# The routing of a mixture-of-experts layer: its work moved between the last tiles of the projection before it, and expert 0 chosen first

## The chip, the cores and the metric

The kernel runs on one core of a Trainium2 chip, as one launch. The metric is the device time of that launch in microseconds, as a median of several runs. TensorE multiplies, VectorE and ScalarE do the elementwise work, the SP queue issues nearly all loads, and GpSimd issues the indirect gathers and scatters of the expert loop. The engines meet at semaphores: an instruction raises a count, another engine's next instruction waits for it.

## What is computed

The reference is a decoder trunk of two layers with a prompt of 256 tokens and 8 samples of 4 tokens, so 288 tokens of 1024 values. Layer 0 has two kinds of attention and a dense SwiGLU, layer 1 two recurrent mixers and a mixture of experts. The change lies between the output projection of layer 1's mixers and its experts. The reference there, shortened:

```python
hp = hp + y                                   # output projection of the mixers, 1536 -> 1024
xn = rms_norm(hp, norm_ffn_odd)
logits = jnp.einsum('btd,de->bte', xn, w_router).astype(jnp.float32)
top_val, top_idx = lax.top_k(logits, TOP_K)   # 2 of 8
top_w = jax.nn.softmax(top_val, axis=-1)
gate = jnp.sum(jax.nn.one_hot(top_idx, N_EXPERTS) * top_w[..., None], axis=-2)
for e in range(N_EXPERTS):
    out = out + gate[..., e:e + 1] * swiglu(xn, we1[e], we3[e], we2[e])   # 1024 -> 3584 -> 1024
```

Everything is float32. Each expert has 44 MB of weights, and the eight of them take more than half of the kernel's time.

## The kernel before

**Layout.** `residual` holds the 288 tokens as columns, in eight chunks of 128 channels. The router and the experts want tokens as rows, in three tiles (`TILES`): 128, 128 and 32 tokens. PSUM has eight banks of 512 columns.

**The projection (`gemm_rows`, L644).** The last call, `_out_odd`, adds up over six halves of weights into eight output tiles, one for each chunk and bank. In the last half every tile m is finished in turn: six matmuls of 288 columns, about 0.8 us, then VectorE adds bank m to `residual` (L745) and raises `added`. `head.follow` (L588) is called behind each tile; before the change it does nothing until the last tile, m = 7.

**The router's head (`RouterHead`, L511).** Behind the last tile TensorE issues, in this order: the scores of chunks 0 to 4 (`score`, L558: 8 experts as weights, 288 tokens as columns, into bank 0), the turns of chunks 0 to 3 (`turn`, L579: three transposes each, to token rows in banks 1 to 3), scores 5 and 6, turns 4 to 6 (banks 4 to 6), then `finish_scores` (L568): for each token tile the seven chunks' partial scores, which VectorE has copied out (`keep_part`), times an identity, plus the last chunk directly. Turn 7 and five warm matmuls follow, which compute nothing that is used. Every float32 matmul is two instructions in the trace, a transpose is one.

**The statistics.** ScalarE squares the turned rows as they come (`square`, L603, 512 columns for each half and token tile, with a running sum). The norm's scale is needed as 1/sqrt(mean), from two ScalarE instructions, logarithm and exponential (L3431, L3433).

**The choice (`choose`, L622).** VectorE copies the logits, compares each expert with each other one (128 x 192 elements), breaks ties by order, counts who is above, and marks the two best in `chosen`. TensorE turns `chosen` into ranks within each expert (L3235 to L3237, matmuls with a triangle and with ones). VectorE makes `at_first` from the ranks of expert 0 (L3284, L3287): for each token a row with 1/rms at its slot among expert 0's 96 slots.

**The picks (L3247).** Expert 0's tokens are not gathered from memory: TensorE multiplies `at_first` with the turned rows. For each of three groups of 32 slots, and each token tile, four matmuls of 256 columns write the four quarters of a bank. VectorE multiplies each group with the norm's gain and transposes it (L3292, L3293) to `item_x`, and raises `half_x` or `xg_ready`.

**The experts (`stage_experts`, L2970).** `open_item` (L3149) begins expert 0 with the first two chunks of its first weight (L3162), group by group, and counts the tokens of all experts (`count`, L3167) ahead of the third group. From the count VectorE works out a table of items for the other experts (L3303 on). `item` (L3172) then runs up products (L3186) and down products (L3202) for each item. Weights come through rings of 8 up slots and 7 down slots: the SP queue issues a load when TensorE has freed its slot (`free_up`, `free_down`). Six up blocks of expert 0 are loaded far ahead (`EARLY_UP`); four down blocks when the last tile is done (`head.all_read`); up slots 6 and 7, and all that SP issues behind them, when `head.chose` and the squares are there (L3084, L3085).

The order on each engine is written by hand, as the order of the calls.

Of the kernel before, what the change touches and what calls it, by code (L numbers as in the profile page):

```python
# [21 lines left out]
ALU = mybir.AluOpType  # L22
ACT = mybir.ActivationFunctionType
# [487 lines left out]
class RouterHead:  # L511


    def __init__(self, k, work, early_up):
# [8 lines left out]
        self.junk = [work[:, n:n + 512] for n in (512, 1024, 1536)]  # L523
# [26 lines left out]
    def weigh(self, dve):  # L550
        gain = self.k.vec[:, VEC["norm_ffn_odd"]:VEC["norm_ffn_odd"] + DC].unsqueeze(2).broadcast_to([P, DC, NE])
        dve.memset(self.sums, 0.0).then_inc(*self.step.up())
# [15 lines left out]
    def finish_scores(self, pe):  # L568
        k = self.k
        pe.wait_ge(*self.part_kept.at(1))  # L570
        pe.wait_ge(*self.added.at(DC))
        for i, (a, n) in enumerate(TILES):
            out = k.ps[0:n, 0, T + NE * i:T + NE * i + NE]
            pe.matmul(out, self.part[:, a:a + n], k.const("ident")[0:NE, 0:NE], start=i == 0, stop=False, skip_group_check=True)
            mm = pe.matmul(out, k.residual[:, DC - 1, a:a + n], self.wr[:, DC - 1, :], start=False, stop=True, skip_group_check=True)
        mm.then_inc(*self.scored.up())
        self.scores_here = self.scored.all()

    def turn(self, pe, c):  # L579
        k = self.k  # L580
        pe.wait_ge(*self.added.at(max(c, 3 if c < 4 else 6) + 1))
# [6 lines left out]
    def follow(self, pe, m):  # L588
        if m < DC - 1:
            return  # L590
        for c in range(5):
            self.score(pe, c)
        for c in range(4):
            self.turn(pe, c)
        self.score(pe, 5)
        self.score(pe, 6)
        for c in range(4, DC - 1):
            self.turn(pe, c)
        self.finish_scores(pe)
        self.turn(pe, DC - 1)  # L600
        self.k.warm(pe, 7, 5)

    def square(self, act, u):  # L603
        if u == 0:
            act.wait_ge(*self.sums_clear)
        for i, (_, n) in enumerate(TILES):
            act.wait_ge(*self.turned_here[u])
            if u:
                act.wait_ge(*self.squared.at(i + 1))
            act.activation(self.junk[i][0:n, :], self.turned_at(i, u), ACT.Square, accum_out=self.sums[0:n, u, i:i + 1]).then_inc(*self.squared.up())  # L610
# [3000 lines left out]
```

## Time and profile before

| what | us |
|---|---|
| median of three runs | 1550.01 (1549.12 to 1551.66) |
| profiled execution, its own time | 1552.72 |
| span of the profiled execution | 1550.8 |
| TensorE matmuls busy | 1523.7 (98%) |
| weight loads busy | 969.0 (62%) |
| VectorE busy | 531.0 (34%) |
| ScalarE busy | 367.6 (24%) |
| last tile of the projection done | 648.95 |
| first pick | 661.28 |
| first matmul of expert 0 | 665.98 |

The profile is of one execution. Times of events count from the start of its span. Busy time of TensorE is modelled: a matmul's duration holds its passage through the array, so successive ones overlap, and the pace is read from the starts or from the chain of waits.

### The profile page before, as it was taken

The page shows a single profiled execution, that of the slowest core. Times are in us where ns is not written, and L with a number is a line of the kernel's source. Part 1 is how long each engine was busy: PE and PEld are TensorE (multiplying, and loading weights), DVE is VectorE, ACT ScalarE, POOL GpSimd, SP SyncE. Part 2 cuts the span into 40 slices and gives each one's busy share as a digit, 9 for nine tenths or more (in the row PEclk, how much of TensorE's full clock was granted, in tenths as well). Part 3 has the DMA queues.
Part 4 walks back from the last instruction along what each step waited for, and adds up shares of the span by engine and source line. Part 5 has one row for each costly group of instructions (what it writes and reads, how often), then busy time and mean ns, then how long its engine had stood idle before and what let it go on. Part 6 is the DMA issues. An engine that isn't in the chain of part 4 may idle for free.

```text
span 1550.8 us, 37362 instructions
## 1 busy us (share of the span) xinstructions
PE 1523.7 (98%) x16815; PEld 969.0 (62%) x16815; DVE 531.0 (34%) x789; ACT 367.6 (24%) x559; POOL 44.9 (3%) x51
## 2 busy tenths in 40 slices
PE   9989999999999999999999999999999999999997
PEld 8976799999999977933533534534435435335344
DVE  5458756663558788541101011011011011010113
ACT  4237544443427577210000000000000000000001
POOL 0000000000000000000000000000000000001000
PEclk9999999999999999999999999999999999999999
DMA  9566555543445382989899999999999999999996
GB/s 354 196 215 217 175 166 171 163 163 137 167 132 196 122 209 71 327 328 421 352 395 413 415 413 417 409 419 415 410 417 418 410 416 416 413 417 414 413 413 233
DMA packets 144488, 479.44 MB, mean 309 GB/s; under 512 B 32184, under 2 KB 61632, under 8 KB 129747
## 3 DMA queue, kind: packets, MB, share of 16 engines
q1 hardware_dynamic: 141404, 469.07, 78.6%
q0 software_dynamic: 2064, 5.66, 0.9%
q8 instruction: 132, 2.16, 0.6%
q10 hardware_dynamic: 871, 2.42, 0.4%
q14 instruction: 17, 0.14, 0.0%
HBM read 463.55 MB, written 13.55 MB: 308 GB/s over the span
## 4 chain that ended last, share of the span: by engine, by line
PE 60%; DVE 0%; ACT 0%; DVEq 0%; issue 0%
PE ps L3186 37%; PE ps L3202 19%; PE ps L507 1%; PE ps L500 1%; PE ps L501 1%; PE ps L3162 0%; PE ps L3247 0%; PE ps L563 0%; PE ps L234 0%; PE ps L3230 0%; PE ps L583 0%; PE ps L3211 0%; PE ps L3218 0%; DVE act L3411 0%; DVE act L3401 0%; DVE tail_rows L3401 0%
## 5 line engine op out<-in xcount | busy, mean ns | idle before, releaser
L3186 PE MATMUL ps<-up_ring,item_x 128*32 128x448 f32 x6000 | 565.6, 539 | 0.0
L3186 PEld LDWEIGHTS ps<-up_ring,item_x 128*32 128x32 f32 x6000 | 194.7, 110 | 365.8 <-issue 364.6
L3202 PE MATMUL ps<-down_ring,hid_t 128*32 128x256 f32 x5376 | 291.5, 379 | 0.0
L3202 PEld LDWEIGHTS ps<-down_ring,hid_t 128*32 128x32 f32 x5376 | 174.7, 110 | 117.9 <-issue 3.9
L3373 DVE TENSOR_TENSOR hid<-hid,ps 128x1344 f32<-128x1344 f32 x16 | 24.9, 1555 | 651.3 <-PE ps L3186 649.9
L490 DVE TENSOR_TENSOR w_lo_dense<-ring,w_hi_dense 128x2048 fp32r<-128x2048 f32 x53 | 121.3, 2291 | 99.6 <-ACT w_hi_dense L484 99.5
L484 ACT CAST w_hi_dense<-ring 128x2048 fp32r<-128x2048 f32 x53 | 100.8, 1902 | 89.5 <-PE ps L507 82.0
L3453 ACT COPY item_y<-ps 128x512 f32<-128x512 f32 x8 | 4.7, 587 | 422.1 <-PE ps L3202 422.1
L1707 PE MATMUL ps<-x_hi_dense,w_hi_dense 128*128 128x288 f32 x352 | 94.9, 299 | 1.8 <-PEq L1594 1.8
L1708 PE MATMUL ps<-x_lo_dense,w_hi_dense 128*128 128x288 f32 x352 | 94.7, 295 | 0.0
L3449 ACT ACTIVATE hid<-ps 128x1344 f32<-128x1344 f32 x16 | 20.7, 1291 | 267.3 <-PE ps L3186 245.7
L500 PE MATMUL ps<-x_hi_dense,w_hi_dense 128*128 128x288 f32 x272 | 73.8, 299 | 0.0
L501 PE MATMUL ps<-x_lo_dense,w_hi_dense 128*128 128x288 f32 x272 | 73.6, 295 | 0.0
L1707 PEld LDWEIGHTS ps<-x_hi_dense,w_hi_dense 128*128 128x128 f32 x352 | 66.2, 188 | 2.0 <-issue 2.0
L1708 PEld LDWEIGHTS ps<-x_lo_dense,w_hi_dense 128*128 128x128 f32 x352 | 66.2, 188 | 0.1
L500 PEld LDWEIGHTS ps<-x_hi_dense,w_hi_dense 128*128 128x128 f32 x272 | 51.2, 188 | 0.5 <-issue 0.5
L501 PEld LDWEIGHTS ps<-x_lo_dense,w_hi_dense 128*128 128x128 f32 x272 | 51.0, 188 | 0.0
L1712 PE MATMUL ps<-x_hi_dense,w_lo_dense 128*128 128x288 f32 x352 | 50.4, 295 | 0.0
L500 PE MATMUL ps<-x_hi_hidden,w_hi_dense 128*128 128x288 f32 x176 | 49.0, 292 | 0.7 <-PEq L1687 0.7
L501 PE MATMUL ps<-x_lo_hidden,w_hi_dense 128*128 128x288 f32 x176 | 48.9, 295 | 0.0
L1712 PEld LDWEIGHTS ps<-x_hi_dense,w_lo_dense 128*128 128x128 f32 x352 | 47.9, 188 | 0.0
L500 PE MATMUL ps<-x_hi_qkv,w_hi_qkv 128*128 128x288 f32 x176 | 47.8, 297 | 0.0
(535 smaller groups left out, 1701.5 us busy)
## 6 DMA issues: line engine op xcount, KB each, us to landing
up_ring<-in_we_dram SPq DMA_DIRECT2D x250, 896.0 KB, 8.6
down_ring<-in_we_dram SPq DMA_DIRECT2D x112, 1024.0 KB, 11.0
ring<-in_w_ffn_dram SPq DMA_DIRECT2D x23, 1024.0 KB, 7.8
ring<-in_w_in_odd_dram SPq DMA_DIRECT2D x9, 2048.0 KB, 8.0
ring<-in_w_in_even_dram SPq DMA_DIRECT2D x5, 2048.0 KB, 15.5
ring<-in_w_ffn_dram SPq DMA_DIRECT2D x5, 2048.0 KB, 7.6
ring<-in_w_out_odd_dram SPq DMA_DIRECT2D x3, 2048.0 KB, 9.0
odd_layer<-in_we_dram SPq DMA_DIRECT2D x6, 896.0 KB, 11.4
```

The source lines that it names most:

```text
L484: act.copy(self.view(self.hi, h), raw).then_inc(*self.hi_done.up())
L490: dve.tensor_tensor(self.view(self.lo, h), self.halves[h][2], self.view(self.hi, h).bitcast(F32), ALU.subtract)\
L500: pe.matmul(out, hi[:, c, cols], x[0][:, r, :], start=first and c == 0, stop=False)
L501: pe.matmul(out, hi[:, c, cols], x[1][:, r, :], start=False, stop=False)
L507: mm = pe.matmul(out, lo[:, c, cols], x[0][:, r, :], start=False, stop=last and c == len(rows) - 1)
L1707: pe.matmul(hidden.bank(m, w), hi[:, c, w, :], x[0][:, c, :], start=c == 0, stop=False)
L1708: pe.matmul(hidden.bank(m, w), hi[:, c, w, :], x[1][:, c, :], start=False, stop=False)
L1712: mm = pe.matmul(hidden.bank(m, w), lo[:, c, w, :], x[0][:, c, :], start=False, stop=c == DC - 1)
L3186: mm = pe.matmul(k.ps[32 * q:32 * q + 32, 3 * w + g, 0:FW], xg[:, c, g, :], block_of[:, q, :], start=c == 0, stop=c == DC - 1, skip_group_ ...
L3202: mm = pe.matmul(k.ps[32 * q:32 * q + 32, 6 + g // 2, 256 * (g % 2):256 * (g % 2) + 256], hidT[:, 2 * r + j, g, :], block_of[:, j, 256 * q ...
L3373: dve.tensor_tensor(hid[:, :, :], hid[:, :, :], k.ps[:, 3:6, 0:FW], ALU.mult).then_inc(mult_done, 1)
L3449: act.activation(hid[:, :, :], k.ps[:, 0:3, 0:FW], ACT.Silu).then_inc(silu_done, 1)
```

## The change

- In the last half of the projection, each tile m from 1 on is followed by the score of chunk m - 1; tiles 5 and 6 are also followed by two turns each (chunks 0 and 1, 2 and 3).
- ScalarE squares each chunk of `residual` (128 x 288) as soon as it is added; VectorE folds the squares chunk by chunk into one tile (`fold`); TensorE sums it over the channels with a column of ones (`sum_squares`), three small matmuls. The squares of turned rows go.
- The logits go to bank 7; the last chunk's part comes first, the partial scores second.
- `choose_first` marks expert 0's tokens alone, from 128 x 24 elements; `rank_first` ranks them. `choose` runs later, behind `at_first`, and its ranks (`rank_all`) are made in `open_item` ahead of the count.
- Turns 4 and 5 stand ahead of `rank_first`, turns 6 and 7 behind it. All seven calls of warm matmuls go.
- ScalarE copies the first half of all three tiles' rows, and the second half of two; VectorE copies the second half of the first.
- The picks run over the first 512 channels of all three groups, then over the second 512: matmuls of 128 columns, twice as many. The tiles are taken in the order 1, 2, 0.
- `open_item` waits for each group by itself; SP waits for the choice only.

The diff, cut to its core:

```diff
     def finish_scores(self, pe):
         k = self.k
+        pe.wait_ge(*self.added.at(DC))
+        scores = [k.ps[0:n, 7, T + NE * i:T + NE * i + NE] for i, (_, n) in enumerate(TILES)]
+        for i, (a, n) in enumerate(TILES):
+            pe.matmul(scores[i], k.residual[:, DC - 1, a:a + n], self.wr[:, DC - 1, :], start=i == 0, stop=False, skip_group_check=True)
         pe.wait_ge(*self.part_kept.at(1))
-        pe.wait_ge(*self.added.at(DC))
         for i, (a, n) in enumerate(TILES):
-            out = k.ps[0:n, 0, T + NE * i:T + NE * i + NE]
-            pe.matmul(out, self.part[:, a:a + n], k.const("ident")[0:NE, 0:NE], start=i == 0, stop=False, skip_group_check=True)
-            mm = pe.matmul(out, k.residual[:, DC - 1, a:a + n], self.wr[:, DC - 1, :], start=False, stop=True, skip_group_check=True)
+            mm = pe.matmul(scores[i], self.part[:, a:a + n], k.const("ident")[0:NE, 0:NE], start=False, stop=True, skip_group_check=True)
         mm.then_inc(*self.scored.up())
         self.scores_here = self.scored.all()
 
+    def sum_at(self, i):
+        return self.k.ps[0:TILES[i][1], 0, T + i:T + i + 1]
+
+    def sum_squares(self, pe):
+        pe.wait_ge(*self.folded.at(DC - 1))
+        for i, (a, n) in enumerate(TILES):
+            mm = pe.matmul(self.sum_at(i), self.sq[0][:, a:a + n], self.k.const("ones")[:, 0:1], start=i == 0, stop=i == 2, skip_group_check=True)
+        mm.then_inc(*self.summed.up())
+        self.sums_here = self.summed.all()
+
     def turn(self, pe, c):
         k = self.k
-        pe.wait_ge(*self.added.at(max(c, 3 if c < 4 else 6) + 1))
         for i, (a, n) in enumerate(TILES):
             mm = pe.transpose(self.turned_at(i, c // 4)[:, P * (c % 4):P * (c % 4) + P], k.residual[:, c, a:a + n], k.const("ident"))
         if c % 4 == 3:
...
     def follow(self, pe, m):
-        if m < DC - 1:
-            return
-        for c in range(5):
-            self.score(pe, c)
-        for c in range(4):
-            self.turn(pe, c)
-        self.score(pe, 5)
-        self.score(pe, 6)
-        for c in range(4, DC - 1):
-            self.turn(pe, c)
-        self.finish_scores(pe)
-        self.turn(pe, DC - 1)
-        self.k.warm(pe, 7, 5)
-
-    def square(self, act, u):
-        if u == 0:
-            act.wait_ge(*self.sums_clear)
-        for i, (_, n) in enumerate(TILES):
-            act.wait_ge(*self.turned_here[u])
-            if u:
-                act.wait_ge(*self.squared.at(i + 1))
-            act.activation(self.junk[i][0:n, :], self.turned_at(i, u), ACT.Square, accum_out=self.sums[0:n, u, i:i + 1]).then_inc(*self.squared.up())
+        if m:
+            self.score(pe, m - 1)
+        if m in (5, 6):
+            self.turn(pe, 2 * m - 10)
+            self.turn(pe, 2 * m - 9)
+        if m == DC - 1:
+            self.finish_scores(pe)
+            self.sum_squares(pe)
+
+    def square(self, act, c):
+        act.wait_ge(*self.added.at(c + 1))
+        if c > 2:
+            act.wait_ge(*self.folded.at(c - 2))
+        act.activation(self.sq[0 if c == 0 else 1 + c % 2], self.k.residual[:, c, :], ACT.Square).then_inc(*self.squared.up())
+        self.squared_here.append(self.squared.all())
+
+    def fold(self, dve, c):
+        dve.wait_ge(*self.squared_here[c])
+        if c > 1:
+            dve.wait_ge(*self.folded.all())
+        if c:
+            dve.tensor_tensor(self.sq[0], self.sq[0], self.sq[1 + c % 2], ALU.add).then_inc(*self.folded.up())
...
-    def keep(self, dve):
-        dve.wait_ge(*self.turned_here[0])
-        for i in range(2):
-            dve.wait_ge(*self.squared.at(i + 1))
-            dve.tensor_copy(self.rows[i][:, 0:512], self.turned_at(i, 0)).then_inc(*self.kept.up())
-
-    def choose(self, dve):
-        k, lg, gt, eq, chosen = self.k, self.lg, self.gt, self.eq, self.chosen
+    def take_mean(self, dve, averaged):
+        dve.wait_ge(*self.sums_here)
+        both = self.k.ps[:, 0, T:T + 2]
+        dve.tensor_scalar(self.sums[:, 0, 0:2], both, 1.0 / D, EPS, ALU.mult, ALU.add).then_inc(*averaged.up())
+        dve.tensor_scalar(self.sums[0:TS, 0, 2:3], self.sum_at(2), 1.0 / D, EPS, ALU.mult, ALU.add).then_inc(*averaged.up())
+
+    def choose_first(self, dve, chose_first):
+        k, lg = self.k, self.lg
 
         def then(ins):
             ins.then_inc(*self.step.up())
             dve.wait_ge(*self.step.all())
         dve.wait_ge(*self.step.all())
         dve.wait_ge(*self.scores_here)
-        dve.tensor_copy(lg[0:TS, 2, :], k.ps[0:TS, 0, T + 16:T + 24]).then_inc(*self.step.up())
-        then(dve.tensor_copy(lg[:, 0:2, :], k.ps[:, 0, T:T + 16].rearrange("p (i e) -> p i e", i=2)))
+        dve.tensor_copy(lg[0:TS, 2, :], k.ps[0:TS, 7, T + 16:T + 24]).then_inc(*self.step.up())
+        then(dve.tensor_copy(lg[:, 0:2, :], k.ps[:, 7, T:T + 16].rearrange("p (i e) -> p i e", i=2)))
+        above, n_above = self.gt[:, :, 0, :], self.eq[:, 0, 0, 0:3]
+        then(dve.tensor_tensor(above, lg[:, :, :], lg[:, :, 0:1].broadcast_to([P, 3, NE]), ALU.is_gt))
+        then(dve.tensor_reduce(n_above, above, AX, ALU.add))
+        valid = k.const("valid").rearrange("p (i e) -> p i e", i=3)
+        dve.scalar_tensor_tensor(self.chosen[:, :, 0], n_above, 2.0, valid[:, :, 0], ALU.is_lt, ALU.mult).then_inc(*chose_first.up())
...
+                if head:
+                    for m in range(DC):
+                        head.square(act, m)
...
+                    if head and 1 <= m < DC - 1:
+                        head.fold(dve, m - 1)
...
                 sp.wait_ge(*head.chose.at(1))
-                sp.wait_ge(*head.squared.at(6))
...
-                        if g == 0:
-                            pe.wait_ge(*half_x.at(3))
+                        if g < 2:
+                            pe.wait_ge(*half_x.at(g + 1))
                         if g == 2:
+                            rank_all()
                             count()
                             pe.wait_ge(xg_ready, 1)
...
+                def rank_first():
+                    pe.wait_ge(*chose_first.at(1))
+                    pe.matmul(first_ranks[:, :], k.const("before"), chosen[:, :, 0], start=True, stop=False, skip_group_check=True)
+                    pe.matmul(first_ranks[:, 1:3], k.const("ones"), chosen[:, 0:1, 0].broadcast_to([P, 2]), start=False, stop=False, skip_group_check=True)
+                    pe.matmul(first_ranks[:, 2:3], k.const("ones"), chosen[:, 1, 0:1], start=False, stop=True, skip_group_check=True).then_inc(*ranked.up())
+
+                def rank_all():
+                    pe.wait_ge(*head.chose.at(1))
+                    pe.matmul(ranks[:, :, :], k.const("before"), chosen[:, :, :], start=True, stop=False, skip_group_check=True)
+                    pe.matmul(ranks[:, 1:3, :], k.const("ones"), chosen[:, 0:1, :].broadcast_to([P, 2, NE]), start=False, stop=False, skip_group_check=True)
+                    pe.matmul(ranks[:, 2, :], k.const("ones"), chosen[:, 1, :], start=False, stop=True, skip_group_check=True)
...
-                pe.wait_ge(*head.chose.at(1))
-                pe.matmul(ranks[:, :, :], k.const("before"), chosen[:, :, :], start=True, stop=False, skip_group_check=True)
-                pe.matmul(ranks[:, 1:3, :], k.const("ones"), chosen[:, 0:1, :].broadcast_to([P, 2, NE]), start=False, stop=False, skip_group_check=True)
-                pe.matmul(ranks[:, 2, :], k.const("ones"), chosen[:, 1, :], start=False, stop=True, skip_group_check=True).then_inc(*ranked.up())
-                k.warm(pe, 1, 2)
+                head.turn(pe, 4)
+                head.turn(pe, 5)
+                rank_first()
+                head.turn(pe, 6)
+                head.turn(pe, 7)
                 pe.wait_ge(*slotted.at(3))
-                for g in range(3):
-                    for i, (_, n) in enumerate(TILES):
-                        if g == 0:
-                            pe.wait_ge(*(head.kept.at(3), copied.at(2), copied.at(3))[i])
-                        by_quarter = rows[i][0:n, :].rearrange("p (c q r) -> p q c r", c=DC, q=4)
-                        for q in range(4):
-                            out = k.ps[32 * q:32 * q + 32, (0, 2, 3)[g], 0:256].rearrange("p (c r) -> p c r", c=DC)
-                            mm = pe.matmul(out, at_first[0:n, i, GROUP * g:GROUP * g + GROUP], by_quarter[:, q, :, :],
-                                           start=i == 0, stop=i == 2, skip_group_check=True)
-                    mm.then_inc(*found.up())
+                for u in range(2):
+                    for g in range(3):
+                        for i in (1, 2, 0):
+                            n = TILES[i][1]
+                            if g == 0:
+                                pe.wait_ge(*((copied.at(3), copied.at(1), copied.at(2)), (head.kept.at(1), copied.at(4), copied.at(5)))[u][i])
+                            by_quarter = rows[i][0:n, 512 * u:512 * u + 512].rearrange("p (c q r) -> p q c r", c=4, q=4)
+                            for q in range(4):
+                                out = k.ps[32 * q:32 * q + 32, (0, 2, 3)[g], 128 * u:128 * u + 128].rearrange("p (c r) -> p c r", c=4)
+                                mm = pe.matmul(out, at_first[0:n, i, GROUP * g:GROUP * g + GROUP], by_quarter[:, q, :, :],
+                                               start=u == 0 and i == 1, stop=u == 1 and i == 0, skip_group_check=True)
+                        if u:
+                            mm.then_inc(*found.up())
...
                 head.keep_part(dve)
-                head.keep(dve)
-                head.choose(dve)
-                dve.wait_ge(*head.squared.at(6))
-                then(dve.tensor_tensor(rstd[:, :], sums[:, 0, :], sums[:, 1, :], ALU.add))
-                dve.tensor_scalar(rstd[:, :], rstd[:, :], 1.0 / D, EPS, ALU.mult, ALU.add).then_inc(*averaged.up())
+                head.fold(dve, DC - 2)
+                head.fold(dve, DC - 1)
+                head.choose_first(dve, chose_first)
+                head.take_mean(dve, averaged)
+                dve.wait_ge(*ranked.at(1))
+                then(dve.scalar_tensor_tensor(spot0[:, :], first_ranks, 1.0, chosen[:, :, 0], ALU.add, ALU.mult))
+                dve.wait_ge(*inverted.at(2))
+                for i in range(3):
+                    dve.tensor_scalar(at_first[:, i, :], slots[:, :], spot0[:, i:i + 1], rstd[:, i:i + 1], ALU.is_equal, ALU.mult).then_inc(*slotted.up())
                 dve.wait_ge(*head.turned_here[1])
                 dve.tensor_copy(rows[0][:, 512:D], head.turned_at(0, 1)).then_inc(*head.kept.up())
-                dve.wait_ge(*ranked.at(1))
-                then(dve.scalar_tensor_tensor(spot0[:, :], ranks[:, :, 0], 1.0, chosen[:, :, 0], ALU.add, ALU.mult))
-                dve.wait_ge(*inverted.at(2))
-                for i in range(3):
-                    dve.tensor_scalar(at_first[:, i, :], slots[:, :], spot0[:, i:i + 1], rstd[:, i:i + 1], ALU.is_equal, ALU.mult)                       .then_inc(*slotted.up())
-                dve.tensor_copy(rank[:, :, :], ranks).then_inc(*half_x.up())
+                head.choose(dve)
                 dve.wait_ge(*head.gains_here)
...
                 dve.wait_ge(*counted.at(1))
+                then(dve.tensor_copy(rank[:, :, :], ranks))
...
-                head.square(act, 0)
-                act.copy(tail[:, 0:512], head.turned_at(2, 0)).then_inc(*copied.up())
-                head.square(act, 1)
-                act.copy(rows[1][:, 512:D], head.turned_at(1, 1)).then_inc(*copied.up())
-                act.wait_ge(*averaged.at(1))
-                act.activation(rstd[:, :], rstd[:, :], ACT.Ln).then_inc(*inverted.up())
+                def take_rows(u, those):
+                    act.wait_ge(*head.turned_here[u])
+                    for i in those:
+                        act.copy(rows[i][:, 512 * u:512 * u + 512], head.turned_at(i, u)).then_inc(*copied.up())
+
+                take_rows(0, (1, 2, 0))
+                act.wait_ge(*averaged.at(2))
+                act.activation(rstd[:, :], sums[:, 0, :], ACT.Ln).then_inc(*inverted.up())
                 act.wait_ge(*inverted.at(1))
                 act.activation(rstd[:, :], rstd[:, :], ACT.Exp, scale=-0.5).then_inc(*inverted.up())
-                act.copy(rows[2][:, 512:D], head.turned_at(2, 1)).then_inc(*copied.up())
+                take_rows(1, (1, 2))
```

## Rows read from the trace of the kernel before

**Rows 1.** one stretch of the time line: busy time of each engine, granted clock, DMA

```profile
690.00:1540.00 850.00, 849.02 (x11326) 368.93 (x11322) 82.13 (x67) 35.23 (x38) 40.72 (x42) 1.00 1.00 407
```

**Rows 2.** the chain of waits: start, us, engine, tile, line, count

```profile
648.95 2.52 PE ps L563 x10
...
651.48 1.46 PE ps L583 x12
...
661.28 4.76 PE ps L3247 x72
...
669.19 0.77 PE ps L3169 x6
...
778.70 72.16 PE ps L3186 x768
...
850.86 36.26 PE ps L3202 x672
```

**Rows 3.** time line, TensorE: start, us, engine, line, operation, tiles, shapes, count

```profile
655.07 0.38 PE L574 MATMUL ps<-core,decay_rows_all 8*128 8x8 f32 x2
...
659.46 0.30 PE L3235 MATMUL ps<-act,core 128*128 128x24 f32 x2
...
665.98 3.21 PE L3162 MATMUL ps<-odd_layer,item_x 128*32 128x448 f32 x32
```

**Rows 4.** time line, VectorE's part in the routing

```profile
648.99 0.46 DVE L745 TENSOR_TENSOR residual<-residual,ps 128x288 f32<-128x288 f32 x1 [0.34 <-PE ps L507]
...
654.04 0.45 DVE L614 COPY decay_rows_all<-ps 8x288 f32<-8x288 f32 x1 [4.32 <-PE ps L563]
...
656.82 0.15 DVE L630 COPY act<-ps 32x8 f32<-32x8 f32 x1 [1.14 <-PE ps L575]
...
657.09 0.36 DVE L634 TENSOR_TENSOR decay_rows_all<-act 128x192 f32<-128x192 f32 x1
...
658.92 0.18 DVE L641 SCALAR_TENSOR_TENSOR act<-act,core 128x24 f32<-128x24 f32 x1
...
660.22 0.16 DVE L3284 SCALAR_TENSOR_TENSOR first_spot<-ps,act 128x3 f32<-128x3 f32 x1 [0.19 <-PE ps L3237]
```

**Rows 5.** time line, TensorE and its weight loads: small matmuls beside the projection's

```profile
180.06 0.38 PE L1075 MATMUL ps<-x_hi_out_even,w_hi_out_even 128*128 128x288 f32 x1
180.28 0.29 PE L1075 MATMUL ps<-x_lo_out_even,w_hi_out_even 128*128 128x288 f32 x1
180.41 0.29 PE L1075 MATMUL ps<-x_hi_out_even,w_hi_out_even 128*128 128x288 f32 x1
...
648.88 0.10 PEld L563 LDWEIGHTS ps<-residual,act 128*8 128x8 f32 x2 [0.17 <-issue]
```

**Rows 6.** time line, ScalarE: one instruction of 512 columns, one of the roots

```profile
566.54 0.61 ACT L2263 ACTIVATE act<-ps 128x512 f32<-128x512 f32 x1
...
659.48 0.20 ACT L3431 ACTIVATE rstd_tokens<-rstd_tokens 128x3 f32<-128x3 f32 x1
```

**Rows 7.** time line, TensorE: 128x32 weights by 128 columns, elsewhere

```profile
550.81 2.19 PE L2434 MATMUL ps<-hgrn_state,q_by_sample 128*32 128x128 f32 x61
```

**Rows 8.** time line: a group's product and transpose, and the first read of slot 6

```profile
663.06 0.42 DVE L3292 TENSOR_TENSOR item_raw<-ps,core 128x256 f32<-128x256 f32 x1 [1.73 <-PE ps L3247]
663.52 0.45 DVE L3293 STREAM_TRANSPOSE item_x<-item_raw 128x256 f32<-128x256 f32 x1
...
680.06 0.13 PEld L3186 LDWEIGHTS ps<-up_ring,item_x 128*32 128x32 f32 x4 [0.25 <-issue]
```

**Rows 9.** four more stretches: busy time of each engine, granted clock, DMA

```profile
98.00:101.00 3.00, 3.00 (x33) 2.78 (x30) 2.97 (x5) 2.71 (x10) 0.00 (x0) 1.00 0.34 131
101.00:105.00 4.00, 2.14 (x18) 1.69 (x17) 3.10 (x8) 2.53 (x9) 0.00 (x0) 1.00 1.00 297
105.00:109.00 4.00, 4.00 (x22) 2.84 (x20) 1.99 (x4) 0.72 (x2) 0.00 (x0) 0.57 0.99 366
654.00:657.00 3.00, 3.00 (x25) 2.62 (x25) 1.82 (x5) 1.32 (x5) 0.00 (x0) 1.00 1.01 429
```

More of the change, by code:

```diff
@@ L522, in __init__ @@
         self.gt, self.eq = (work[:, 192 * n:192 * n + 192].rearrange("p (i e f) -> p i e f", i=3, e=NE) for n in range(2))
-        self.junk = [work[:, n:n + 512] for n in (512, 1024, 1536)]
+        self.sq = [work[:, n:n + T] for n in (512, 1024, 1536)]
+        self.folded, self.summed, self.squared_here = k.count("sq"), k.count("sum"), []
         self.turned_here = []
@@ L551, in weigh @@
         gain = self.k.vec[:, VEC["norm_ffn_odd"]:VEC["norm_ffn_odd"] + DC].unsqueeze(2).broadcast_to([P, DC, NE])
-        dve.memset(self.sums, 0.0).then_inc(*self.step.up())
+        dve.memset(self.sums, 1.0).then_inc(*self.step.up())
         dve.memset(self.lg, 0.0).then_inc(*self.step.up())
@@ L614, in keep_part, with then @@
         dve.tensor_copy(self.part, self.k.ps[0:NE, 0, 0:T]).then_inc(*self.part_kept.up())
-    def keep(self, dve):
-        dve.wait_ge(*self.turned_here[0])
-        for i in range(2):
-            dve.wait_ge(*self.squared.at(i + 1))
-            dve.tensor_copy(self.rows[i][:, 0:512], self.turned_at(i, 0)).then_inc(*self.kept.up())
+    def take_mean(self, dve, averaged):
[5 more added lines that the diff above has]
+        k, lg = self.k, self.lg
+        def then(ins):
+            ins.then_inc(*self.step.up())
+            dve.wait_ge(*self.step.all())
+        dve.wait_ge(*self.step.all())
+        dve.wait_ge(*self.scores_here)
+        dve.tensor_copy(lg[0:TS, 2, :], k.ps[0:TS, 7, T + 16:T + 24]).then_inc(*self.step.up())
[5 more added lines that the diff above has]
+        dve.scalar_tensor_tensor(self.chosen[:, :, 0], n_above, 2.0, valid[:, :, 0], ALU.is_lt, ALU.mult).then_inc(*chose_first.up())
     def choose(self, dve):
@@ L627, in then @@
             dve.wait_ge(*self.step.all())
-        dve.wait_ge(*self.step.all())
-        dve.wait_ge(*self.scores_here)
-        dve.tensor_copy(lg[0:TS, 2, :], k.ps[0:TS, 0, T + 16:T + 24]).then_inc(*self.step.up())
-        then(dve.tensor_copy(lg[:, 0:2, :], k.ps[:, 0, T:T + 16].rearrange("p (i e) -> p i e", i=2)))
         other = lg[:, :, :].unsqueeze(2).broadcast_to([P, 3, NE, NE])
@@ L3034, in stage_experts @@
         half_x, tabled, xn_made, dve_step = (k.count(x) for x in ("placed", "taps", "tokens_copied", "dve_step"))
+        chose_first = k.count("shifted_s")
         cleared, zeros_in, diagonal, spread, own_made, combined = (k.count(x) for x in (
@@ L3048, in stage_experts @@
         ranks = k.ps[:, 7, T:T + 24].rearrange("p (i e) -> p i e", i=3)
+        first_ranks = k.ps[:, 7, T + 32:T + 35]
         with k.stage(within) as block:
@@ L3165, in open_item @@
                                 mm.then_inc(up_used, 1)
+                def rank_first():
[8 more added lines that the diff above has]
+                    pe.matmul(ranks[:, 2, :], k.const("ones"), chosen[:, 1, :], start=False, stop=True, skip_group_check=True)
                 def count():
                     for i in range(3):
-                        mm = pe.matmul(k.ps[:, 7, T + 32:T + 32 + NE], k.const("ones"), chosen[:, i, :], start=i == 0, stop=i == 2)
+                        mm = pe.matmul(k.ps[:, 7, T + 32:T + 32 + NE], k.const("ones"), chosen[:, i, :], start=False, stop=i == 2, skip_group_check=True)
                     mm.then_inc(*counted.up())
@@ L3296, in _ @@
                     else:
-                        dve.wait_ge(*half_x.at(3))
+                        dve.wait_ge(*half_x.at(2))
                         ins.then_inc(xg_ready, 1)
@@ L3404, in mean @@
                     n = TILES[j][1]
-                    dve.wait_ge(*squared.at(6 + j + 1))
+                    dve.wait_ge(*squared.at(j + 1))
                     dve.tensor_scalar(stat[0:n, j, 0:1], stat[0:n, j, 0:1], 1.0 / D, EPS, ALU.mult, ALU.add).then_inc(*ready.up())
```

## The prediction

> **What bounds the kernel now.** I read the page's busy shares first (TensorE 98%), then the stretches, then the chain of waits, and only then the time line of the routing. The stretch from 690 to 1540 is 850 us in which TensorE is busy for 849 [rows 1]: it is the bound there, and in the chain every expert costs the same two terms, 72.16 and 36.26 us, one behind the other [rows 2]. The DMA share in it is 1.00 at 407 GB/s, so the transfers run close behind, but TensorE's waits name no DMA there: a later or earlier start of the experts moves the end by just that much. The change touches nothing in this stretch. So the question is one interval: from the end of the out projection's last tile (648.95) to the opening matmuls of expert 0 (L3162, from 665.98), and what is put between those. Before, it is 17.0 us: 12.3 to the first pick at 661.28 and 4.7 of picks (661.28 to 665.98) [rows 2, 3]. What ends last within the 12.3 us is a relay: scores, VectorE's choice (656.82 to 659.10), ranks on TensorE, VectorE's slots (660.22 to 661.23), picks [rows 3, 4]. ScalarE's squares and the turned rows (tiles transposed by TensorE) lie beside it, and 14 warm matmul instructions fill TensorE's wait (the code, L600 and L3238).
>
> I write t0 for the end of the out projection's last tile in the new kernel.
>
> **1. Work put between the last tiles.** Six scores and four turns (three transposes each) now stand ahead of the last tile, where nothing waits for them: TensorE is never idle there, so each delays t0 in full. Five scores took 2.52 us, 0.50 each, and four turns 1.46 [rows 2]. That alone is 3.0 + 1.5 = 4.5. Then each switch between the two kinds of matmul: the first score's weight load stood idle for 0.17 us, and after such a block the projection's own matmuls start again with a step of 0.22 us (180.06 to 180.28) where the next is 0.13 [rows 5]. I count 0.09 for each way. Six scores at 0.49 + 0.18, turns 1.46 and two more switches of 0.09 make 5.6, which I take since rows 5 show this alternation; the lower end is 4.5, the upper 6. t0 = 648.95 + 5.6 = 654.55. The added folds on VectorE (0.46 each by the 128x192 rows of 0.36 and the 0.46 residual add) and squares on ScalarE (at most the 0.61 of 512 columns, for 288) fit in a tile's period of 0.8 to 1.4 us beside the add [rows 4, 6]. Were VectorE late, its add would still only be needed at t0.
>
> **2. From t0 to the first pick.** TensorE: score 6 to t0+0.6; the last chunk's scores need the last add (t0+0.5) and end at t0+1.4. VectorE: add, scan, copy of the partial scores (0.45) until t0+1.2 [rows 4]. TensorE's three partial-score products follow, t0+2.2: all six pairs took from 655.07 to the copy at 656.82 [rows 3, 4], half of it is 0.87. VectorE meanwhile does its two last folds until t0+2.2, so the squares' sum is ready for TensorE just when that ends; six tiny matmuls again, to t0+3.1. VectorE chooses expert 0 alone: two copies 0.27, then three instructions of 24 columns or fewer at 0.21 with their hand-over, t0+3.2. This replaces the six 128x192 instructions that stood from 657.09 to 658.92 [rows 4]: 1.2 us less here. Mean to t0+3.5; ScalarE's two activations, 0.2 each plus hand-over, t0+4.0 [rows 4, 6]. TensorE: turns 4 and 5 until t0+3.8 (0.37 each), expert 0's ranks until t0+4.6 (0.76 from the first start to L3284, which waits for them, before) [rows 3, 4]. VectorE: slots, 1.06 from L3284's start to the pick's start before, t0+5.7. Turns 6 and 7 end at t0+5.3, inside this wait. So t0+5.7 against 12.3: 6.6 us less, and 5.6 of it is paid in step 1. Picks start at 660.25, 1.0 earlier. Ends: 5.3 (each hand-over 0.05 shorter) to 7 (one further hand-over of each engine and the turns in the way of the ranks).
>
> **3. Picks by halves.** Before, 72 instructions of 256 columns took 4.70 us, 65 ns each [rows 2, 3]. Now 144 of 128 columns. The columns are as many, but what surrounds them is not. The same form, 128x32 weights and 128 columns into four quarters, runs elsewhere as 61 in 2.19 us, the last one's own 0.28 included: 32 ns each [rows 7]. And a round of 24 picks took 1.57 us (4.70 by 3), where the experts' pitch for 256 columns, 54 ns (36.26 by 672), gives 1.29 [rows 2]: 0.28 is lost in a round, which I put down to its two passages, to the 32-row tail and back. There were three rounds, now six. Six rounds of 24 x 0.032 + 0.28 = 1.05 make 6.3 us: 1.6 more. Ends: 4.6 (144 x 0.032, passages hidden) and 9.4 (144 at the old 65 ns). I take 6.3, by the row of the very shape. The second half's rows are there in time: turned at t0+5.3, ScalarE's two copies at 0.56 end at t0+6.5, VectorE's 0.68 at t0+6.4; the second half is read from t0+8.8.
>
> **4. The full choice moves behind the slots.** VectorE copies rows (0.68) and then chooses for all experts (2.2 by rows 4: 656.82 to 658.92 and the last hand-over) until t0+8.6; the first finished pick group comes at about t0+9.9, so nothing queues behind it. The three products and transposes (0.92 each [rows 8]) then end at t0+10.9, 11.9 and 13.0. Opening matmuls start at t0+12.0 and want the third at t0+16: hidden with 2 us to spare. The opening's first two groups took 3.2 [rows 3]. SP's queue waits for the full choice before it loads up slots 6 and 7: about 663.1 instead of right behind the choice at 659.10. Behind it stand only loads that TensorE's own progress releases, and slot 6 is first read at 680.06 [rows 8], 17 us later. The four down loads that follow the last tile go 5.6 us later, for the down products behind all of expert 0's up products. No cost; if the cover went, the wait for slot 6 would be what shows.
>
> **5. Full ranks move into the opening.** Six more matmul instructions stand ahead of the count. The count's six cost 0.77 in the chain [rows 2], the ranks' 0.57. I take 0.65; 0.3 to 1.0.
>
> **Sum.** Before 17.0; now 5.6 + 5.7 + 6.3 + 0.65 = 18.25. So 1.2 us later, and the rest unchanged. The profiled execution took 1552.72 (span 1550.8, 1.9 around it) and would become 1553.9; it lies 2.7 above the median of the three, and I take the difference to the median: 1550.0 + 1.2 = **1551.2**. With every low end, -2.3; with every high end, +6.4.
>
> **Rivals.**
> *The clock falls (slower).* Place: the picks and the opening. The new interval has no warm matmuls: from t0+0.5 to t0+5.7 TensorE runs 24 instructions of 1 to 8 columns, 12 transposes and a 0.4 us wait. For it: the granted clock fell at 105 from its upper to its lower level (2.4 to 1.2 GHz; 0.57 is the mean of the 4 us), after a stretch in which TensorE was busy 2.14 of 4 us, almost all of it transposes [rows 9]. Against: at 98 to 101 transposes alone kept 1.00, and 654 to 657, as thin as the new interval, kept it too, though warm matmuls followed [rows 9]. Price: a mean of 0.57 over 4 us is 3.4 us at half; 3.4 us at half speed lose 1.7. Total +2.9, **1552.9**; twice that length gives +4.6. It decides as soon as the fall comes before the picks end. The Trainium skill (TensorE: Matmul & The Clock Gate, Part 4) says that transposes do not count as activity as matmuls do; by that rule the 12 transposes protect nothing. The trace agrees at 105 and does not at 98.
> *Half-width picks cost as much as full ones.* 144 x 65 ns = 9.4, 3.1 more than taken: +4.3, **1554.3**. For it: before, the picks ran at 65 ns where the experts' same form runs at 54. Against: the 32 ns row of the same shape [rows 7]. The same title's section "Back-to-back issue gap" gives about 81 ns for each pair of weight load and 128-column matmul; by it the picks would be 11.7 us and the total +6.6, **1556.6**. Rows 7 contradict it for quarter tiles.
> *The switches and passages are free (faster).* 4.5 in step 1 and 4.6 in step 3: 1.2 - 1.1 - 1.7 = -1.6, **1548.4**. For it: passages before may be a property of the 256-column groups. Against: rows 5.
> *It doesn't do what it says:* the last folds or the roots rather than the choice hold the slots; this is step 2's upper end, 1.3 more, +2.5: **1552.5**. It is held in the forecast's share.
>
> **Chances.** Forecast with its bounds (-0.5 to +2.6) 0.5; clock 0.27; full-price picks 0.08; free switches 0.15. A measurement of this kernel tells no less than 0.2% (3.1 us), its three runs lying 2.5 us apart. Faster by more than that takes all low ends and a lucky run: 0.08. Slower: a third of the clock's share, nearly all of the full-price picks, and some of the forecast's tail: 0.18. Same: 0.74. The range, 1548.3 to 1554.8, holds from the free switches to a long drop.
>
> **What would show it.** The last tile ends at about 654.5 and each score between tiles costs 0.67; first pick at 660.2; picks last 6.3 us; L3162 starts at 666.5; each expert keeps 72.16 and 36.26. A granted clock below 1.00 between 655 and 670 shows the clock rival. Wrong would be a wait of the experts' matmuls for a DMA, or an opening that starts before 664 or after 669.

## The result, and the profile after

The changed kernel took 1555.92 us (median of 16 runs, 1550.73 to 1562.27) and the kernel before 1551.39 on the same chip (16 runs, 1548.28 to 1554.94): a ratio of 1.0031, interval 1.002 to 1.0042, so 4.8 us slower by the ratio, 4.5 by the medians. The forecast was 1.2 us slower, 1551.2, and its range ended at 1554.8: wrong. Of the 4.7 us between forecast and measurement, 1.4 are the kernel before itself, whose three runs had given 1550.01; the 4.8 us of slowing are at the far end of what the range allowed, four times the forecast's.

The profiled execution took 1557.95, 2 us above the median (span 1556.1 against 1550.8 before). The page's first rows and the strip of the granted clock:

```profile
span 1556.1 us, 37514 instructions
PE 1528.7 (98%) x16885; PEld 972.5 (62%) x16885; DVE 532.7 (34%) x797; ACT 368.7 (24%) x557; POOL 45.0 (3%) x51
PEclk9999999999999999989999999999999999999999
```

The clock row, a 9 everywhere in the page of before, has an 8 here, in the slice of the routing. The chain of waits of the changed kernel (start, us, engine, tile, line) from the out projection's tile 1 to the experts:

```profile
641.84 0.58 PE ps L564 x2
642.42 0.33 PE ps L500
...
648.72 0.81 PE ps L594 x6
...
652.24 0.27 PE ps L507 x2
...
654.59 0.76 PE ps L587 x6
655.35 1.15 PE ps L594 x6
656.50 0.22 PE ps L3199 x2
656.72 0.43 PE ps L3200 x2
657.14 0.42 PE ps L3201 x2
657.57 1.38 PE ps L594 x6
658.95 9.72 PE ps L3291 x144
668.67 5.08 PE ps L3192 x32
...
675.19 1.64 PE ps L3192 x16
...
783.93 72.16 PE ps L3228 x768
856.10 36.26 PE ps L3244 x672
```

The reader is to see three things. The experts' terms, 72.16 and 36.26, are those of [rows 2] to the hundredth. The first pick starts 6.4 us behind the last tile's end (652.51) and no longer 12.3. And the picks take 9.72 where [rows 2] have 4.76, the opening's first two groups 5.08 where the chain of before has 3.14:

```profile
666.05 3.14 PE ps L3162 x32
```

The windows of the changed kernel (stretch, its length, busy time of each engine, PEclk, DMA share, GB/s) say why:

```profile
641.80:652.50 10.70, 10.70 (x62) 6.77 (x62) 4.57 (x11) 2.88 (x7) 0.00 (x0) 1.00 0.29 119
652.50:658.90 6.40, 6.32 (x41) 5.07 (x42) 3.74 (x17) 2.27 (x6) 0.00 (x0) 0.75 0.85 317
658.90:668.40 9.50, 9.50 (x145) 4.71 (x148) 4.22 (x11) 1.05 (x2) 0.00 (x0) 0.50 1.00 410
668.40:675.10 6.70, 6.70 (x52) 2.75 (x44) 1.57 (x3) 0.00 (x0) 0.00 (x0) 0.68 0.05 20
```

The granted clock is 1.00 between the last tiles, falls at 655.7 (0.83 from 655 to 656), is 0.50, the lower of its two levels (1.2 GHz), through all the picks, and comes back at 672.7, in the opening. That is 17 us, in most of which TensorE was busy without a gap.

It isn't the same in each execution. The changed kernel's 16 runs had mean granted clocks from 0.990 to 0.998. The two with 0.998 took 1551.48 and 1550.73, the three with 0.990 took 1560.94, 1562.27 and 1561.46. I call (1 - mean clock) x 2 x time a run's low time, the microseconds it would have spent at half speed: 19.5 us in the mean here, and a straight line through the 16 runs rises 0.43 us for each of them. For the 16 runs of the kernel before beside them no clocks are on record.

### The profile page after: what moved, and what is told of

It reads as the page before. It is cut to its first block, busy times and chain, and to the rows that moved or that the text cites. A ratio compares the mean times of both kernels' runs of the same rounds, so it can differ in the third digit from the quotient of the medians.

```text
span 1556.1 us, 37514 instructions
## 1 busy us (share of the span) xinstructions
PE 1528.7 (98%) x16885; PEld 972.5 (62%) x16885; DVE 532.7 (34%) x797; ACT 368.7 (24%) x557; POOL 45.0 (3%) x51
## 4 chain that ended last, share of the span: by engine, by line
PE 60%; DVE 0%; ACT 0%; DVEq 0%; issue 0%
PE ps L3228 37%; PE ps L3244 19%; PE ps L500 1%; PE ps L507 1%; PE ps L501 1%; PE ps L3291 1%; PE ps L3192 0%; PE ps L594 0%; PE ps L564 0%; PE ps L3272 0%; PE ps L3253 0%; PE ps L3260 0%; DVE act L3456 0%; DVE act L3446 0%; DVE tail_rows L3446 0%; DVEq L3533 0%
```

## The experiments

Kernels of one group ran on one chip and share its runs of the kernel before: e1 to e4 (before: 1558.74, 31 runs, mean low time 10.6), e5 to e8 (1557.48, 28 runs, 8.2), e9 to e11 (1559.06, 24 runs, 9.8). My theory: the change takes out the warm matmuls, the clock falls. The rival: half-width picks cost more, at any clock.

**e1, the kernel before without its warm matmuls.** 14 instructions are gone.

```
         self.turn(pe, DC - 1)
-        self.k.warm(pe, 7, 5)
...
-                k.warm(pe, 1, 2)
                 pe.wait_ge(*slotted.at(3))
```

> The kernel before with both groups of warm matmuls taken out of the routing (14 instructions) and nothing else. Clock theory: with them gone TensorE has only small matmuls and transposes from 654 to 661, the granted clock falls there in most executions, and the time rises by 2 to 5 us; the picks of 256 columns then run at about twice 65 ns. Work theory (the change is slow because it added instructions): the warm matmuls stood in waits, so the time stays within 0.5 us and the clock at 1.00.

1563.91 (8 runs), ratio 1.0039 (1.0024 to 1.0054), so 6 us slower; mean low time 24.6 against 10.6, no run's clock above 0.995. One slope laid through the runs of both kernels, 0.38 us for each microsecond of low time, leaves 0.2 us of difference at equal low time (about 0.9 either way): the low time is the whole of it. The windows, and the chain's picks and opening groups:

```profile
655.00:672.00 17.00, 13.93 (x103) 4.79 (x106) 7.10 (x21) 3.12 (x10) 0.00 (x0) 0.51 0.50 193
```

```profile
659.58 8.69 PE ps L3245 x72
668.27 5.23 PE ps L3161 x32
```

Taking the warm matmuls away is enough for the same 17 us at the lower level, and picks of full width then take 8.69 instead of 4.76. The clock is low through picks of either width.

**e2, the changed kernel with warm matmuls put back**, four instructions ahead of the squares' sums and six ahead of the wait for the slots.

```
             self.finish_scores(pe)
+            self.k.warm(pe, 0, 2)
             self.sum_squares(pe)
...
                 head.turn(pe, 7)
+                pe.wait_ge(*averaged.at(2))
+                k.warm(pe, 0, 3)
                 pe.wait_ge(*slotted.at(3))
```

> The changed kernel with five calls of warm matmuls put back: two between the scores and the squares' sum, three ahead of the wait for the slots (behind the mean's two instructions, so that bank 0 is free). Clock theory: the granted clock stays at 1.00 from 655 to 673, the picks take 6.3 to 7 us instead of 9.7, the opening's two groups 3.1 instead of 5.1; the warm calls cost up to 2 us of their own, and the time is 1.5 to 3.5 us above before, instead of 4.8. Work theory: the changed kernel's time plus what the warm calls cost, 5 to 7 us above before.

1560.09 (12 runs), ratio 1.0014 (1.0 to 1.0027); mean low time 11.7, at the level of before on the same chip (10.6). The windows and the chain:

```profile
657.00:673.00 16.00, 16.00 (x227) 9.92 (x226) 9.48 (x31) 3.33 (x8) 0.00 (x0) 1.00 0.93 377
```

```profile
664.24 5.69 PE ps L3294 x144
669.93 3.01 PE ps L3193 x32
```

The clock stays at its upper level (2.4 GHz), picks by halves take 5.69 and the two opening groups 3.01. What is left, 1.4 us by the medians and 2.2 by the ratio, is what the change and the added ten instructions cost at full clock: in this profile tile 1's end to the third opening group is 27.99 us, in the one of before 25.74.

**e3, the kernel before with picks by halves** (the pick loop of the changed kernel, its rows all waited for at their first use).

```
-                for g in range(3):
-                    for i, (_, n) in enumerate(TILES):
...
+                for u in range(2):
+                    for g in range(3):
+                        for i in (1, 2, 0):
...
```

> The kernel before with its picks by halves alone (144 instructions of 128 columns in the new order of tiles, all rows waited for as before). Clock theory with the prediction's sizes: the clock stays at 1.00 ahead of the picks as before, the picks take 6.3 us instead of 4.7, time +1.6 us. If half-width picks cost as much as full ones: 9.4 us, +4.7. If half-width picks do not hold the clock: it falls during them or behind them, and the time rises by 3 us or more, with a wide spread.

1559.94 (12 runs), ratio 1.0022 (1.0007 to 1.0036), mean low time 11.5 against 10.6: 1.2 us by the medians, 3.4 by the ratio. A round of 24 picks takes 0.925 us, six of them 5.6 against 4.7. The profile also has a pause near the end of the picks, for which it shows no cause and which the one of before lacks:

```profile
663.10 0.97 issue
```

So halves cost about one microsecond at full clock by their pace, and here perhaps one more by such a pause; they aren't what lets the clock fall (1.00 from 650 to 675).

**e4, the changed kernel with picks of full width** (the loop of before back in its place).

> The changed kernel with its picks over the whole width again (72 instructions of 256 columns, once all rows are there, about 1 us later). Clock theory: the fall at 655 is the same, since it comes before the picks. If the half-width picks are what keeps the clock down for 16 us, it now rises some 3 to 7 us earlier and the time is 2 to 4 us above before; if any picks keep it down, the picks take about 8 us and the time is 4 to 6 us above before. Work theory: the halves' 1.6 us go, +3.

1561.94 (12 runs), ratio 1.0016 (0.9999 to 1.0033), mean low time 16.7. Its profiled execution fell too:

```profile
660.00:674.00 14.00, 13.10 (x99) 3.94 (x102) 6.67 (x18) 1.05 (x2) 0.00 (x0) 0.52 0.84 353
```

```profile
661.86 8.69 PE ps L3289 x72
670.54 4.93 PE ps L3192 x32
```

So the half-width picks are not what holds the clock down. Two of its runs had a clock of 0.999 and took 1555.80 and 1556.86; the three runs of the kernel before at 0.999 took 1554.96, 1556.36 and 1556.48.

**e5, the changed kernel again, nothing changed,** to see an execution in which the clock doesn't fall.

> The changed kernel, unaltered, beside the other kernels of this call. Clock theory: each microsecond at half clock costs 0.4 to 0.5 us, as the executions of the first four experiments show (0.37 to 0.47 over their mean clocks), so executions near a mean clock of 0.998 lie 1 to 3 us above before's at the same clock, and most lie lower in clock and 5 us above; median +4 to +6 us. Work theory: the 4.8 us stay at equal clock.

1562.91 (8 runs), ratio 1.0038 (1.0023 to 1.0054): the result repeats on another chip; mean low time 18.8 against 8.2. This time the profiled execution, the fastest of the eight, kept the clock in the routing (mean 0.998, span 1555.6). Its chain and its windows:

```profile
651.75 0.27 PE ps L507 x2
...
656.26 0.17 DVE first_spot L3326
656.46 0.82 DVE at_first L3329 x3
657.32 5.76 PE ps L3291 x144
663.08 3.43 PE ps L3192 x32
666.50 0.33 PE ps L3205 x2
...
667.27 0.67 PE ps L3211 x6
667.94 1.64 PE ps L3192 x16
```

```profile
652.00:657.30 5.30, 4.85 (x39) 3.83 (x38) 3.78 (x18) 2.60 (x7) 0.00 (x0) 1.00 0.80 294
657.30:662.90 5.60, 5.58 (x145) 3.20 (x146) 3.82 (x11) 0.72 (x2) 0.00 (x0) 1.00 1.01 424
662.90:667.90 5.00, 5.00 (x56) 2.59 (x48) 1.79 (x4) 0.00 (x0) 0.00 (x0) 1.00 1.00 415
```

Same program, same instructions, and the picks take 5.76 where the other execution shows 9.72. This is the trace to hold the working against.

**e6, warm matmuls and picks of full width together** (the edits of e2 and e4).

> The changed kernel with five warm calls (two ahead of the squares' sum, three ahead of the slots) and picks over the whole width. Clock theory: clock at 1.00 from 655 to 673, mean low time as before; picks 4.7 us; time 0.5 to 1.5 us above before, at least 3 us below the changed kernel. Work theory: 4 us above before.

1560.44 (8 runs), ratio 1.0024 (1.0012 to 1.0035), mean low time 12.1: 3.0 us above before, where 0.5 to 1.5 was expected, and with more low time than before's 8.2. In the profile the clock is 1.00 from 650 to 672, and it is still slower than before: the work between the tiles puts the last tile's end 5.9 us later and shortens what follows, up to the third opening group, only from 21.01 to 16.47.

**e7, e6 with the scores and turns back behind the last tile,** the expert-0-first choice and the folds kept.

```
-        if m:
-            self.score(pe, m - 1)
-        if m in (5, 6):
-            self.turn(pe, 2 * m - 10)
-            self.turn(pe, 2 * m - 9)
...
+        for c in range(5):
+            self.score(pe, c)
+        self.turn(pe, 0)
+        self.turn(pe, 1)
+        self.score(pe, 5)
+        self.score(pe, 6)
+        self.turn(pe, 2)
+        self.turn(pe, 3)
+        self.finish_scores(pe)
+        self.k.warm(pe, 0, 2)
+        self.sum_squares(pe)
```

> As the kernel with whole-width picks and five warm calls, but nothing between the tiles: scores and turns stand behind the last tile (scores 0 to 4, turns 0 and 1, scores 5 and 6, turns 2 and 3). If the switches between tiles cost about 0.2 us each as the trace shows, this gains 1.1 to 1.7 us over e6 and is level with before or up to 1 us faster, the clock at 1.00. If interleaving was free, the chain to the slots is longer than in e6 and nothing is gained.

1556.49 (11 runs), ratio 0.9994 (0.9986 to 1.0003), mean low time 6.2. From its windows and chain:

```profile
645.00:668.00 23.00, 23.00 (x213) 12.93 (x216) 11.57 (x42) 3.93 (x10) 0.00 (x0) 1.00 0.70 267
```

```profile
645.63 2.52 PE ps L564 x10
...
657.23 4.69 PE ps L3296 x72
661.92 3.14 PE ps L3197 x32
...
666.50 1.64 PE ps L3197 x16
```

Five scores in a row take 2.52, as in [rows 2], where each of those between tiles lengthened the tile's period from 0.79 to 1.57. The last tile to the third opening group takes 20.87, before 21.01: level, and 1.5 us less than e6 from tile 1's end on. The rest of the 4 us between the medians of e6 and e7 goes with their low time, 12.1 and 6.2.

**e8, e6 with only the four warm instructions ahead of the squares' sums.**

> The changed kernel with whole-width picks and only the two warm calls ahead of the squares' sum. If these two are enough to hold the clock, the time is about 1 us below e6, close to before. If the clock still falls in a share of the executions, behind the last turns and the wait for the slots, the median lies 2 to 3 us above before with a spread of 8 us or more.

1560.92 (12 runs), ratio 1.0021 (1.0006 to 1.0035), mean low time 14.8. That is between e6's 12.1 and e5's 18.8, but these means are uncertain by 2 to 3 us each and don't separate the three. The profile does:

```profile
655.00:672.00 17.00, 16.12 (x115) 7.08 (x119) 6.97 (x20) 1.46 (x4) 0.00 (x0) 0.51 0.79 317
```

TensorE was busy for 16.12 of these 17 us, and the clock was low all the same. The four instructions end at 655.00 in its chain and the clock falls half a microsecond later: they don't hold it in this execution.

**e9, e7 with six warm instructions in place of ten** (`warm(pe, 0, 1)` and `warm(pe, 0, 2)`).

> The kernel of e7 with three warm calls instead of five (one ahead of the squares' sum, two ahead of the slots). At full clock the shorter relay saves 0.5 us ahead of the sum and up to 0.5 us ahead of the picks, so 0.5 to 1 us below e7 and 1 to 2 us below before. If three calls don't hold the clock, executions with a fall appear that e7 does not have, and the median lies above e7's.

1559.81 (12 runs), ratio 1.0003 (0.999 to 1.0016), mean low time 14.1. In its trace, with the clock at 1.00 from 645 to 668, the last tile to the third opening group took 20.07, 0.9 less than before; it isn't faster, probably because of its low time, 14.1 against before's 9.8, a difference of twice its uncertainty.

**e10, the changed kernel with eight warm instructions between the two halves of the picks,** to see what brings a low clock back.

```
                 for u in range(2):
+                    if u:
+                        k.warm(pe, 7, 4)
                     for g in range(3):
```

> The changed kernel with four warm calls between the two halves of its picks: behind the fall, not ahead of it. They cost 2 us at full clock and 4 at half. If the picks and small matmuls are what keeps the clock down once it has fallen, the warm calls end the low time some 5 to 8 us earlier (9 to 12 us of it instead of 17), and the executions with a fall gain about 3 us and pay 2 to 4: total 4 to 7 us above before, with a smaller mean low time than the changed kernel's 19 us. If the low time has its own fixed length of 17 us whatever runs, it stays, and the time is 7 to 9 us above before.

The windows and the chain:

```profile
658.00:668.00 10.00, 9.72 (x88) 5.34 (x88) 3.35 (x11) 1.05 (x2) 0.00 (x0) 0.53 1.01 424
668.00:672.00 4.00, 4.00 (x81) 1.92 (x84) 2.02 (x5) 0.00 (x0) 0.00 (x0) 0.88 0.51 207
```

```profile
659.31 5.01 PE ps L3293 x72
664.32 4.14 PE ps L234 x8
668.46 3.14 PE ps L3293 x72
671.60 3.01 PE ps L3192 x32
```

In this execution the low stretch lasts 10 us, from 658.7 to 668.9, not 17: it ends half a microsecond behind the warm instructions, and the second half of the picks, the same 72 instructions, takes 3.14 where the first took 5.01. In time it lost: 1567.95 (7 runs), ratio 1.0054 (1.0035 to 1.0073), 8.9 us where I had expected 4 to 7, and the mean low time over its runs, 22.0, is no shorter than the 18.8 of e5, on another chip. One profile shows the length of one fall; how often falls come I had wrong, and that stays open.

**e11, e7 once more** on this chip.

> The kernel of e7 unaltered, to see whether its 1 us less than before (ratio 0.9994, interval 0.9986 to 1.0003) repeats on this chip: expected ratio 0.9990 to 1.0003, mean low time no longer than before's. If the earlier gain was chance, the ratio lies at 1.000 or above.

1559.56 (12 runs), ratio 1.0003 (0.9989 to 1.0016), mean low time 9.9. The small gain of e7 isn't repeated: no version beats the kernel before.

## Why the prediction was wrong

The steps, each against the profiled executions; e5 is the changed kernel at full clock. Terms are read from the chains' rows; the last tile's end is the end of its last L507.

| step | predicted | e5 | changed, clock fallen |
|---|---|---|---|
| 1 work between the tiles | 5.6 | 5.9 | 5.9 |
| 2 last tile to the first pick (before 12.3) | 5.7 | 5.3 | 6.4 |
| 3 picks (before 4.8) | 6.3 | 5.8 | 9.7 |
| 4 the full choice hidden | 0 | 0 | 0 |
| 5 full ranks in the opening | 0.65 | 0.77 | 0.77 |

**Step 1** was right in kind and a little small: tile 1's end to tile 7's is 10.67 us in e5 and 4.74 before, 5.9 for six scores and four turns, where each score costs 0.79 and not the 0.67 I took. **Step 2** came out at the low end, 5.30. **Step 3**: a round of 24 half-width picks takes 0.925, not 1.05, so 0.16 is lost in each round and not 0.28; 144 in 5.76 is 40 ns each, and the rival of full price, 65 ns, is refuted. **Step 4**: the loads of up slots 6 and 7 leave SP's queue at 661.63 in the changed kernel, 663.1 predicted,

```profile
661.63 0.33 SPq L2979 DMA_DIRECT2D up_ring<-in_we_dram  x1
```

and from 668 to 800 no matmul waits for anything that the profile shows. **Step 5** is a tenth more, and the two opening groups take 3.43 where e7 has 3.14 and e2 3.01: 0.3 that I didn't have.

From tile 1's end to the third opening group this makes 25.74 us before, 26.59 in e5: 0.85 more, where the sum had 1.2. **The sum was right for an execution in which the clock stays up,** by some luck: its terms were off by 0.1 to 0.5 us each, in both directions. Most executions don't keep the clock. In the profile of the changed kernel the same interval is 33.35, 6.76 more than in e5, in steps 2, 3 and the opening (1.14, 3.96 and 1.66).

**The step that failed is the clock rival's term and its chance.** I named the mechanism, the place, the missing warm matmuls, and then took its length, 3.4 us, from the stretch at 105 [rows 9]: 1.7 us lost. It lasted 17 us and cost 6.76. The row at 105 is not a freak: every fall from 100 to 118, near 200 and near 555 in the thirteen profiles lasted 3.4 us. But the routing's fall did not: 17 us here, in e1 and in e8, 13.6 in e4, 10.2 in e10. The clock stayed at its lower level through 9.5 us of unbroken picks. Nor was 3.4 us the only length in the trace of before: from 9 to 17 the mean was 0.57 over 8 us, which is 6.9 at half, with TensorE busy throughout (last section), and the prediction does not use it. Why the fall in the routing is longer stays open; that small work follows it there is argued, and one execution (e10) speaks for it. The doubling that I allowed came to 3.4 us of loss, half of what it cost.

The chance was wrong too: 0.27 for something that happens in some six of ten runs, an estimate from 10.6 us more low time than before on the chip of e5 and 17 us for a fall. By profiles: of the six without warm matmuls ahead of the wait for the slots (the changed kernel, e1, e4, e5, e8, e10) five had the fall, of the seven with them (before, e2, e3, e6, e7, e9, e11) none. "654 to 657, as thin as the new interval, kept it too, though warm matmuls followed" was the decisive half-sentence. Those matmuls were the reason, as e1 shows by removing nothing but them (1.0039), and e2 by putting ten instructions back (mean low time 11.7, before's on that chip 10.6; the changed kernel itself has 19.5 and 18.8, though on other chips).

The result splits like this: 0.85 us of the change's own work, and 10.6 us more low time in a run than before (18.8 against 8.2 on the chip of e5) at some 0.4 us each, 4.2 us. Together 5.1; measured on that chip were 5.4 by the medians and 5.9 by the ratio, and 4.8 in the result. One slope through both kernels' runs there (0.42) leaves 0.7 us at equal low time, about 0.7 either way. The split rests on averages over a clock given to three digits (0.001 is 3 us of low time), and a part of the low time lies elsewhere than in the routing; e1 and e2 carry the cause, the split only its size.

The Trainium skill (TensorE: Matmul & The Clock Gate, Part 1) says that the ramp penalty is under 1% of a typical kernel's span. The traces agree in size, 6.76 us being 0.43% here; it is most of what the change lost all the same. The rule about transposes in Part 4 of that page, which the prediction weighed, no run here tested alone.

What stays open: what in the routing lets the clock fall in one execution and keeps it in the next (the changed kernel kept it in e5's profile and lost it in its own), and why e10's runs had no less low time than e5's.

## What to carry to other kernels

Matmuls that compute nothing may be what holds the clock: before a change removes them, price the whole of the small work that follows at the lower level, not only the length of a fall seen elsewhere. Compare executions at equal mean clock; the time alone mixes the work and the fall. And small float32 matmuls moved between large ones of another type (float32r in the code) cost their switch each time: 0.79 us a score here, 0.50 in a row. What is moved is better kept together; no run here tried a block ahead of the last tile.

## What was not expected of the hardware

TensorE at 0.50 of its clock while busy for 9.50 of 9.50 us, and at 0.51 for 17 us while busy for 16.12 (e8): in these stretches being busy didn't bring the clock back. It rose in the opening's matmuls of 448 columns (the changed kernel, e1, e4, e8), and in e10 among the half-width picks, half a microsecond behind the warm instructions.

Low stretches come in one execution of a kernel and not in the next, early in the kernel too: from 9 to 17 the profiled execution of the kernel before had 0.57 and that of the changed kernel 1.00, as the windows of the one and of the other show. Its interval of the routing is 7.6 us longer and its span only 5.3: the 2.3 between them were gained ahead of the routing, for which this stretch is the one difference of the clock that I found.

```profile
9.00:17.00 8.00, 8.00 (x31) 5.97 (x31) 5.75 (x10) 6.57 (x11) 0.00 (x0) 0.57 1.08 368
```

```profile
9.00:17.00 8.00, 7.98 (x51) 6.57 (x52) 6.49 (x13) 6.61 (x11) 0.00 (x0) 1.00 1.08 367
```
